# The second feed-forward product of a decoder trunk, summed form by form in PSUM

## What is computed

```python
x = layer_norm(ALPHA * x + mix, ln1_g[i], ln1_b[i])
hid = square(relu(x @ ffn_w1[i]))                 # 1024 x 4096
x = layer_norm(ALPHA * x + hid @ ffn_w2[i], ln2_g[i], ln2_b[i])
gate = sigmoid(x @ ple_gate_w[i])
x = x + gate * (p[i] @ ple_w[i])
```

## Time and profile before

| what | value |
|---|---|
| median of 3 runs | 2134.86 us (2134.71 to 2137.01) |
| the profiled execution's own time | 2136.69 us |
| its span in the trace | 2134.9 us |
| granted TensorE clock, mean | 0.999 of full |
| busy: TensorE, VectorE, GpSimd, ScalarE | 99%, 65%, 46%, 36% |
| matmuls | 10613 |
| moved by DMA | 233.87 MB, 110 GB/s on average |

### The profile page before, as it was taken

One profiled execution on the slowest core, in us unless ns is written; L12 is line 12 of the kernel. 1 busy time (PEld: TensorE's weight loads), 2 busy tenths in 40 slices (PEclk: granted clock), 3 DMA queues, 4 the chain that ended last, 5 costly groups with the idle time before them and its releaser, 6 DMA issues.

```text
span 2134.9 us, 28066 instructions
## 1 busy us (share of the span) xinstructions
PE 2115.5 (99%) x10613; PEld 1796.4 (84%) x10613; DVE 1396.5 (65%) x1991; ACT 776.6 (36%) x1185; POOL 992.4 (46%) x597
## 2 busy tenths in 40 slices
PE   9999999999999999999999999999999999999999
PEld 9887788888878888899888888888888878888899
DVE  5744775556698888675543353676555798788774
ACT  3112455444543333521211101554445533333521
POOL 5113167777655546112422223258877655556120
PEclk9999999999999999999999999999999999999999
DMA  5111124434655443201121111024444664443211
GB/s 184 40 60 51 29 80 153 153 138 154 209 201 177 138 168 99 79 26 45 40 79 40 60 40 55 25 87 155 157 154 144 211 200 165 138 168 104 65 38 72
DMA packets 150018, 233.87 MB, mean 110 GB/s; under 512 B 11169, under 2 KB 80893, under 8 KB 149885
## 3 DMA queue, kind: packets, MB, share of 16 engines
q1 hardware_dynamic: 149184, 231.78, 32.6%
q10 hardware_dynamic: 700, 0.31, 0.1%
HBM read 172.28 MB, written 59.77 MB: 109 GB/s over the span
## 4 chain that ended last, share of the span: by engine, by line
PE 88%; DVE 6%; POOL 2%; issue 2%; ACT 1%; DVEq 0%; ACTq 0%; POOLq 0%
PE bank_a L1763 15%; PE bank_a L1765 15%; PE bank_a L1764 15%; PE bank_b L1763 14%; PE bank_b L1765 14%; PE bank_b L1764 14%; POOL op_lo L942 1%; PE bank_a L1802 1%; DVE resid L1520 1%; DVE xt_lo L1314 1%; POOL op_sum L1015 1%; PE bank_b L1802 1%; DVE xt_hi L1309 1%; DVE resid L1551 0%; PE bank_a L1978 0%
## 5 line engine op out<-in xcount | busy, mean ns | idle before, releaser
L927 POOL TENSOR_TENSOR w_lo<-raw,w_hi 128x512 fp32r<-128x512 f32 x160 | 223.4, 1426 | 674.8 <-ACT w_hi L1036 674.7
L1763 PE MATMUL bank_a<-xt_hi,w_hi 128*128 128x512 f32 x640 | 251.4, 393 | 2.7 <-DVE xt_lo L1314 2.7
L1765 PE MATMUL bank_a<-xt_hi,w_lo 128*128 128x512 f32 x640 | 249.2, 389 | 0.0
L1764 PE MATMUL bank_a<-xt_lo,w_hi 128*128 128x512 f32 x640 | 249.1, 389 | 0.0
L969 POOL TENSOR_TENSOR wop_lo<-w_sum,wop_hi 128x1024 fp32r<-128x1024 f32 x56 | 135.3, 2416 | 231.7 <-ACT wop_hi L1143 231.7
L1763 PE MATMUL bank_b<-w_hi,xt_hi 128*128 128x256 f32 x640 | 182.7, 285 | 2.7 <-DVE xt_lo L1314 2.3
L1036 ACT CAST w_hi<-raw 128x512 fp32r<-128x512 f32 x160 | 88.3, 620 | 255.8 <-PE bank_a L1765 154.7
L1765 PE MATMUL bank_b<-w_hi,xt_lo 128*128 128x256 f32 x640 | 181.1, 283 | 0.0
L1764 PE MATMUL bank_b<-w_lo,xt_hi 128*128 128x256 f32 x640 | 181.1, 283 | 0.0
L1763 PE MATMUL bank_b<-wop_hi,hop_hi 128*128 128x512 f32 x464 | 180.8, 390 | 0.0
L1765 PE MATMUL bank_b<-wop_hi,hop_lo 128*128 128x512 f32 x464 | 180.6, 389 | 0.0
(11 more groups left out here) (188 smaller groups left out, 5364.8 us busy)
## 6 DMA issues: line engine op xcount, KB each, us to landing
h_raw<-h_spill SPq DMA_DIRECT2D x106, 512.0 KB, 3.7
h_spill<-h_tile SPq DMA_DIRECT2D x170, 256.0 KB, 2.1
w_raw<-in_ffn_w_dram SPq DMA_DIRECT2D x64, 512.0 KB, 5.4
w_raw<-in_ffn_w_dram SPq DMA_DIRECT2D x112, 256.0 KB, 3.5
raw<-in_od_w_in_dram SPq DMA_DIRECT2D x48, 256.0 KB, 2.9
raw<-in_ple_gate_w_dram SPq DMA_DIRECT2D x32, 256.0 KB, 3.0
h_spill<-h_tile2t SPq DMA_DIRECT2D x28, 256.0 KB, 2.0
raw<-in_ev_w_in_dram SPq DMA_DIRECT2D x24, 256.0 KB, 3.1
```

Of the source, the lines that this page charges most:

```text
L927: pool.tensor_tensor(w_lo[slab % 2][:, s], raw[:, n % NRAW, :], w_hi[slab % 2][:, s].bitcast(F32), ALU.subtract).then_inc(lo_split, 1)
L1763: pe.matmul(dst, s_hi, m_hi, start=first, stop=False, skip_group_check=on_top)
L1764: pe.matmul(dst, s_hi, m_lo, start=False, stop=False, skip_group_check=on_top)
L1765: return pe.matmul(dst, s_lo, m_hi, start=False, stop=last, skip_group_check=on_top)
```

## The change

`ORDER` and its loop over pairs are gone. All eight pairs, the plain blocks' too, go through the scheme. `ITEMS` has 56 items: m1 of eight pairs, then m6 and m2 in turn for eight pairs, then m5, m3, m7 and m4 with eight pairs each. A form's eight products are summed in PSUM and read out once. m6, m5 and m3 go on top of m1's banks, m4 on top of m7's, so that the sums of Winograd's form arise in the banks; `resid` gets each when its form is done. The last two items run together, tile by tile.

Pair 0, of the plain blocks, gets its sums h1 to h4 in the new stages `psum_in` (SyncE loads four tiles of 512 KB), `psum` (VectorE, four additions) and `psum_out` (SyncE stores four). The weights are loaded by quarter: one transfer of 512 KB in half rows for each form and pair, three for m6; eight in a ring, then four for m4. `t2_of` keeps the sum t2 of each pair's weights. The low part of h is always GpSimd's, the low part of the weights always VectorE's. There are five slots; items 52 to 55 have `LAST_SLOTS`. The stages `fold` and `wide` are gone, the `common` tile too.

```diff
-PAIRS = (FFN_BLOCKS - PLAIN) // 2
-ORDER = ("m1", "m5", "m2", "m3", "m7", "m6", "m4")
...
-H_LOW_DVE = (1, 4, 6)
...
+PAIRS = FFN_BLOCKS // 2
+FORMS = dict(m1=("A", 0, ("b11",), 0), m6=("A", 5, ("b12", "b11", "b22"), 2), m5=("A", 4, ("b22",), 1),
+             m3=("A", 6, ("b22",), 0), m2=("B", 1, ("b21",), 0), m7=("B", 2, ("b11",), 1), m4=("B", 3, ("b21",), 1))
+ITEMS = ([("m1", j) for j in range(PAIRS)] + [(form, j) for j in range(PAIRS) for form in ("m6", "m2")]
+         + [(form, j) for form in ("m5", "m3", "m7", "m4") for j in range(PAIRS)])
+ON_TOP = ("m6", "m5", "m3", "m4")
+LAST_FORM = len(ITEMS) - PAIRS
+LAST_SLOTS = (3, 4, 0, 1, 3, 4, 0, 3)
...
+        for i in range(-1, n):
+            if i + 1 < n:
+                dve += FORMS[ITEMS[i + 1][0]][3]
+                self.sum[i + 1] = dve
+            if i >= 0:
+                self.hop_low.append(n * layer + i + 1)
+                dve += 1
                 self.dve.append(dve)
...
+        return i % 5 if i < LAST_FORM else LAST_SLOTS[i - LAST_FORM]
...
+    def hop_chunk(i):
+        return (192, 196, 48, 52)[i % 4] if i < LAST_FORM else (192, 196, 200)[(i - LAST_FORM) % 3]
...
+    def w_chunk(self, load):
+        if load < self.first_load[LAST_FORM]:
+            return (184, 188, 32, 36, 168, 172, 176, 180)[load % 8]
+        return (128, 132, 168, 172)[(load - self.first_load[LAST_FORM]) % 4]
...
+    def w_user(self, load):
+        i = max(i for i in range(len(ITEMS)) if self.first_load[i] <= load)
+        if ITEMS[i][0] == "m6":
+            return self.sum[i]
+        return self.dve[i]
+    def w_before(self, load):
+        return next((k for k in range(load - 1, -1, -1) if self.w_chunk(k) == self.w_chunk(load)), None)
...
+            if b == last and op in ("S2", "A12", "S4", "S3"):
+                prepare(layer, ("S2", "A12", "S4", "S3").index(op))
+        a, nxt, heads = ahead[layer], 4, {}
+        ln = 2 * layer + 1
+        for i, (form, j) in enumerate(ITEMS):
+            while i and nxt < len(ITEMS) and (a.user_before(nxt) is None or a.user_before(nxt) < i):
+                prepare(layer, nxt)
                 nxt += 1
-            st = add("prod", item=i, layer=layer)
+            st = add("prod", item=i, layer=layer, head=heads.get(form))
+            if j == 0:
+                heads[form] = st
             if i == 0:
...
                 step(len(tr.seq) - 1)
...
                 add("lasthid", layer=layer)
...
+            if i in (1, 2, 3):
+                add(("psum_in", "psum", "psum_out")[i - 1], layer=layer)
+            if i == LAST_FORM - PAIRS:
+                squares_of(lo)
+            if i == LAST_FORM - PAIRS + 2:
+                add("stats", half=0, ln=ln)
+                add("norm", half=0, ln=ln)
+            if i == LAST_FORM:
+                turns("ln", 0, [0, 1, 2, 3], ln=ln, layer=layer)
+            if i == LAST_FORM + 1:
+                turns("ln", 0, [4, 5, 6, 7], ln=ln, layer=layer)
+            if i == LAST_FORM + 3:
+                add("slab", layer=layer, load_next=True, split_next=True)
+            if i == LAST_FORM + 5:
+                add("second", layer=layer)
+        st.inner = [add("turn_p", half=0, layer=layer, nested=True, early=True)]
+        squares_of(hi).inner = st.inner
+        add("stats", half=1, ln=ln)
+        add("norm", half=1, ln=ln)
...
+    def prepare(layer, n):
+        if n + 1 < len(ITEMS):
+            add("wsum", item=n + 1, layer=layer)
+        add("prep", item=n, layer=layer)
...
+            def load_item(layer, i):
+                a, last = ahead[layer], FFN_BLOCKS - 1
+                form, _ = ITEMS[i]
+                p, role = a.pair(i), FORMS[form][1]
+                if a.hop_before(i) is not None:
+                    sp.wait_ge(ahead_pool, a.hop_low[a.hop_before(i)])
+                elif i >= 4:
+                    sp.wait_ge(ahead_pool, a.hop_low[i - 4])
+                if p:
+                    sp.wait_ge(spill_out[role], a.spilled(role, 2 * p + 1))
+                elif form in ("m1", "m2", "m4"):
+                    sp.wait_ge(spill_out[role], a.spilled(role, 1))
                 else:
...
+                    sp.wait_ge(first_out, 64 * (layer + 1))
+                slot, _ = a.hop_landed(i)
+                src = h_dram[layer, 2 * p:2 * p + 2, role].rearrange("k p s -> p k s")
+                sp.dma_start(h_raw[a.hop_chunk(i)][:, :, :], src).then_inc(h_in[slot], 16)
+                for n, quarter in enumerate(FORMS[form][2]):
+                    load = a.first_load[i] + n
+                    before = a.w_before(load)
+                    if before is not None:
+                        sp.wait_ge(ahead_dve, a.w_user(before))
+                    elif load == 4:
+                        sp.wait_ge(trip_done, trips[layer].done[last, "S3"])
+                    f, half = int(quarter[1]) - 1, int(quarter[2]) - 1
+                    rows = ffn_w2[layer][2 * p * BLK:(2 * p + 2) * BLK, half * HALF:(half + 1) * HALF]
+                    rows = rows.rearrange("(c f p) n -> p c f n", c=2, f=2, p=P)
+                    slot, _ = a.w_landed(load)
+                    sp.dma_start(w2_raw[a.w_chunk(load)][:, :, :], rows[:, :, f, :]).then_inc(w2_in[slot], 16)
...
                             sp.wait_ge(op_low, tr.lo[b, "A22"])
...
                             sp.wait_ge(acc_ready, st.accd)
...
+                            load_item(layer, 0)
+                            load_item(layer, 1)
                         if (b, op) == (last, "A11"):
                             sp.wait_ge(trip_done, tr.done[b, op])
...
+                            load_item(layer, 2)
+                            load_item(layer, 3)
...
                 if st.kind == "lasthid":
                     layer, b = st.layer, FFN_BLOCKS - 1
                     tr = trips[layer]
                     sp.wait_ge(squares_made, tr.quarter[b, "c21"])
                     spill(layer, b, 1, h_tile1[b % 2])
-                    load_ahead(layer, 6)
+                    load_item(layer, 4)
+                    load_item(layer, 5)
                     for name, role in (("h1", 4), ("h2", 5), ("h3", 2)):
                         sp.wait_ge(hid_step, tr.hid[b, name])
                         spill(layer, b, role, h_tile[role] if role > 3 else h_tile2)
...
                     sp.wait_ge(hid_step, tr.hid[b, "h4"])
                     spill(layer, b, 6, h_tile[6])
...
+                    load_item(layer, 6)
+                    load_item(layer, 7)
+                if st.kind == "psum_in":
+                    a = ahead[st.layer]
+                    for role in range(N_ROLES):
+                        sp.wait_ge(spill_out[role], a.spilled(role, FFN_BLOCKS - 1))
+                    sp.wait_ge(trip_done, trips[st.layer].done[FFN_BLOCKS - 1, "A22"])
+                    for role in range(4):
+                        sp.dma_start(first_h[role][:, :, :], h_dram[st.layer, 0:2, role].rearrange("k p s -> p k s"))\
+                            .then_inc(first_in, 16)
+                if st.kind == "psum_out":
+                    for role, tile, count in ((4, 3, 1), (2, 2, 2), (5, 0, 3), (6, 1, 4)):
+                        sp.wait_ge(first_step, 4 * st.layer + count)
+                        sp.dma_start(h_dram[st.layer, 0:2, role].rearrange("k p s -> p k s"), first_h[tile][:, :, :])\
+                            .then_inc(first_out, 16)
+                if st.kind == "prep" and st.item >= 4 and st.item + 4 < len(ITEMS):
+                    load_item(st.layer, st.item + 4)
...
+                    pool.wait_ge(ahead_hi, a.act[i] - 1)
+                    pool.tensor_tensor(hop_lo[k][:, :, :], h_raw[a.hop_chunk(i)][:, :, :],
+                                       hop_hi[k][:, :, :].bitcast(F32), ALU.subtract).then_inc(ahead_pool, 1)
...
+                    a, i = ahead[st.layer], st.item
+                    k, form = a.slot(i), ITEMS[i][0]
+                    if a.user_before(i) is not None:
+                        name, value = item_done(a, a.user_before(i))
                         act.wait_ge(sem_of[name], value)
                     else:
...
+                        act.wait_ge(trip_done, trips[st.layer].done[FFN_BLOCKS - 1, ("S1", "S2", "A12", "S4", "A22")[i]])
+                    slot, landed = a.hop_landed(i)
                     act.wait_ge(h_in[slot], landed)
...
+                    act.copy(hop_hi[k][:, :, :], h_raw[a.hop_chunk(i)][:, :, :]).then_inc(ahead_hi, 1)
+                    if FORMS[form][3]:
+                        act.wait_ge(ahead_dve, a.sum[i])
+                    else:
+                        slot, landed = a.w_landed(a.first_load[i])
+                        act.wait_ge(w2_in[slot], landed)
+                    act.copy(wop_hi[k][:, :, :], w2_source(a, i)).then_inc(ahead_hi, 1)
...
+                if st.kind == "psum":
+                    c11, c21, c12, c22 = [h[:, :, :] for h in first_h]
+                    dve.wait_ge(first_in, 64 * (st.layer + 1))
```

(65 more changed lines are left out.)

391 lines of the change are left out of this document (96 added, 295 removed).

## The result

| | before | after |
|---|---|---|
| median, runs of the comparison | 2135.94 us (4 runs, 2134.71 to 2137.11) | 2193.85 us (4 runs, 2191.59 to 2194.04) |
| ratio after/before | | 1.0269, 95% interval 1.0251 to 1.0287 |
| span in the trace | 2134.9 us | 2192.1 us |
| granted TensorE clock, mean | 0.999 | 0.988 |
| matmuls | 10613 | 10565 |

A forecast was written before the change was run, and what follows sets the result against it. TensorE's instruction stream and its pauses bound the kernel. Pauses, clock and end less matmuls and old pauses gave +22.4 us in layer 0 and +20.8 in layer 1, +43.2 on 2134.86: 2178 us, range 2146 to 2198.

The forecast's parts named there:

- Matmuls: Second feed-forward product: 1344 matmuls per layer for 1368, 24 fewer, -5.44 us per layer.
- The start: Start of the second product, queues ordered anew: three pauses of TensorE, 27.6 us per layer, item 8 beginning at 648.4.
- A22's wait: First pause: the first product's last step waits for VectorE's c22 sum behind preparations 1 and 2, 2.5 us.
- The second and third pause: Item 7 waits behind VectorE's psum, 11.6 us; item 8 for m1's banks, behind item 12's weights, 13.5 us.
- Clock: After the long pauses at the start: low TensorE clock costs 1.6 us, once per layer, between nothing and twice this.
- The end: End of the second product: preparation 55 and last norm with less cover, 0 to 3 us per layer, taken as 1.0.
- Steady work: VectorE and GpSimd need at most 4.8 of 5.44 us per item, hidden by four products of lead; costed at nothing.
- The third rival: More pauses in the middle, VectorE or GpSimd losing 0.3 us per item: 2192 us or more; chance 0.12.
- The first rival: Pauses at the psum wait don't come, first_in landing before 609.1: 15.2 us faster, 2120 us; chance 0.07.
- the 1.6 us of layer 1's clock: Low clock after layer 1's 1.82 us pause in the kernel before: counted as a saving of 1.6 us, once.
- The rule of the Trainium skill on transfer size: Weights loaded by quarter: skill wants 1 MiB or more per DMA; set aside for a trace row at 403 GB/s.

The follow-up runs named there:

- c4: Changed kernel with start and end reordered, all hop_lo on VectorE, and the psum group after products 4, 8 and 9: 2119.55 us, ratio 0.9922.
- a2: Changed kernel with psum_in, psum and psum_out after products 3, 8 and 9 in place of 1, 2 and 3: 2175.90 us, ratio 1.0182.
- a4: Changed kernel with c22's sum ahead of preparation 2, and preparation 3 behind lasthid: 2183.73 us, ratio 1.0221.
- a1: Changed kernel with the sums of item 12's weights behind m1's flush in VectorE's order: 2181.62 us, ratio 1.0213.

## Why the prediction was right, and where it was short

*Matmuls.* As forecast: 48 fewer of 0.227 us, 10.9 us.

*The start.* Right in mechanism, and in layer 0 in size. A22's wait was 2.4 and 3.1 us (forecast 2.5), first_h landed at 620.5 (620.7), item 7 resumed at 629.1 (629.5), item 12's weights landed at 644.1 (644.1), item 8 began at 648.4 (648.4). The queue moved 387 to 395 GB/s at 600 to 620 where 385 was taken, but 351 at 630 to 640, and only the 0.4 us that item 7 was early made up for it: that the last two agree to a tenth is luck. The second and third pause measured 11.1 and 12.0 where 11.6 and 13.5 were forecast: the idle time is counted from the modelled end of a matmul, and item 7 ran partly at the low clock, which shortened the third. Against c4, which has none of the pauses, item 8 starts 27.8 us late in layer 0 (648.43 for 620.62; forecast 27.6). In layer 1 it loses 30.0 us, measured from behind the last norm of layer 0: A22's wait is 3.1 there, and matmuls of 0.63 us behind it show the low clock, which the forecast did not have at this place. a2, a4 and a1 showed each wait to come from the place it was put at; a1 added that VectorE's backlog is a second bound, 5.3 us short of the first.

*Clock.* Short. Forecast 1.6 us per layer, with what follows the second pause hidden. From 648.43 to 653.18 eleven matmuls began where 11 x 0.227 = 2.50 us would do: 2.25 us; in layer 1, fourteen from 1794.22 to 1800.17 give 2.8. After the norm, 12 matmuls and 16 transposes took 4.73 us (931.55 to 936.28) in layer 0, in c4 3.24: 1.5 us more. In layer 1 the clock did not fall there.

*The end.* The term that was sized wrong: "between nothing and 3 us per layer; I take 1.0". From item 8's first matmul to the first transposes behind the last norm the changed kernel takes 931.55 - 648.43 = 283.1 us, c4 896.40 - 620.62 = 275.8; the 7.3 us are 2.3 of low clock behind the start, 2.0 for wop_lo 55, 1.8 more for the norm (2.50 less c4's 0.66), and a rest of 1.2 that I did not take apart. With the 1.5 behind the norm the end cost 6.5 us in layer 0. In layer 1 the same stretch takes 283.9 against 275.8; less the 2.8 of low clock, the end cost 5.3. So 11.8 us stand against the forecast's 2.0: 9.8 of the 14.0 us that the spans differ from the forecast by. The clock behind the start has 1.9 of them and the start of layer 1 2.4.

I had counted item 55's own 4.7 us against 5.44, but not what stands ahead of it and of the norm. On ScalarE a cast that waits for a transfer stands ahead of hop_hi 55 and five more ahead of the squares; on GpSimd w_lo of the gate slab stand ahead of hop_lo 55, themselves late by the 9.0 us of hop_lo 53. That is what the forecast asked of the start (what is queued ahead, on each engine) and not of the end.

*Steady work.* Costed at nothing, rightly: no wait between item 9 and item 54. The third rival did not come. The working was too kind to itself all the same: m6 has two sums and not one, so its item needs up to 2.4 + 1.2 + 2.4 = 6.0 us of the two engines in turn, more than a product's 5.44; m6 and m2 together need 9.7 of 10.9, and the lead held.

*Two slips in the working.* The first rival says that 6.6 MB are queued ahead of the four loads. By the forecast's own list it is 10.75 less 2.1, that is 8.65 MB; 6.6 leaves out item 8's four transfers, and the true figure speaks more strongly against that rival. And the 1.6 us of layer 1's clock were taken off a median of 2134.86, although all executions of the kernel before up to 2135.4 us have a mean granted clock of 1.0, and those from 2136.4 up, the profiled one among them, 0.999 or less. Without that the forecast would have been 1.6 us higher.

*The rule of the Trainium skill on transfer size* (DMA: Bandwidth & Descriptors, Measured) was set aside by the row of before; the windows above, 387 to 395 GB/s in transfers of 512 KB, bear that out.

## What to carry to other kernels

When loads or weights are brought in a new order, add up the bytes ahead of each transfer that an in-order engine waits for: that gave the landings of layer 0 to within 0.2 us, and moving those waits behind work already supplied won 45 us with no operation changed. Do the same sum at the end of the stage as at its start, on every engine's queue, and expect a second bound behind each wait that you remove. Which engine forms an operand mattered little for the pauses of the start; at the end it cost 11 us, through what stood ahead in the queues and through the waits of GpSimd and VectorE for each other.
